# Rows of the earlier expert block fetched during the last block, last block's y added by a gate matrix, in a fused mixer and grouped-MoE layer

## What is computed

```python
    logits = (xt @ w_router).astype(jnp.float32) + router_bias.astype(jnp.float32)
    probs = jax.nn.softmax(logits, axis=-1)
    grp = probs.reshape(-1, N_EXPERT_GROUPS, EXPERTS_PER_GROUP)
    grp_score = lax.top_k(grp, TOP_K)[0].sum(-1)
    g_idx = lax.top_k(grp_score, 1)[1][:, 0]
    ...
    top_w, top_i = lax.top_k(jnp.where(emask, probs, -1.0), TOP_K)
    top_w = top_w / jnp.sum(top_w, axis=-1, keepdims=True)
    ...
    for e in range(N_EXPERTS):
        h = jax.nn.silu(xt @ w_gate[e]) * (xt @ w_up[e])
        y = y + gates[:, e:e + 1] * (h @ w_down[e])
```

## Time and profile before

| what | us |
|---|---|
| median of 3 runs (691.17 to 695.81) | 694.7 |
| the profiled execution | 699.86 |
| its span | 698.0 |
| TensorE busy | 665.8 |
| VectorE busy | 506.0 |
| ScalarE busy | 345.7 |
| GpSimd busy | 133.6 |

### The profile page before, as it was taken

One profiled execution on the slowest core, in us unless ns is written; L12 is line 12 of the kernel. 1 busy time (PEld: TensorE's weight loads), 2 busy tenths in 40 slices (PEclk: granted clock), 3 DMA queues, 4 the chain that ended last, 5 costly groups with the idle time before them and its releaser, 6 DMA issues. The chain is left out here.

```text
span 698.0 us, 9606 instructions
## 1 busy us (share of the span) xinstructions
PE 665.8 (95%) x3815; PEld 560.5 (80%) x3815; DVE 506.0 (72%) x583; ACT 345.7 (50%) x342; POOL 133.6 (19%) x80
## 2 busy tenths in 40 slices
PE   6999999988999999999969999999999999999796
PEld 5999899988997887577858888888888888888531
DVE  4226446799667384767695999999999999999536
ACT  4538412312227241011506787777787777777202
POOL 0000524332031210400020111111111111100064
PEclk9999999999999999999899999999999999999897
DMA  8951111201612105079247999999999999993173
GB/s 285 382 196 61 61 61 61 89 34 61 183 59 86 53 16 193 0 212 413 106 184 285 371 406 397 416 414 411 409 409 406 407 411 414 413 387 116 62 252 132
DMA packets 48689, 162.56 MB, mean 233 GB/s; under 512 B 4294, under 2 KB 23450, under 8 KB 36364
## 3 DMA queue, kind: packets, MB, share of 16 engines
q1 hardware_dynamic: 41756, 136.62, 51.4%
q0 software_dynamic: 6896, 25.43, 9.4%
HBM read 142.61 MB, written 19.44 MB: 232 GB/s over the span
## 5 line engine op out<-in xcount | busy, mean ns | idle before, releaser
L1338 DVE TENSOR_TENSOR RA<-FA,RA 128x2048 fp32r<-128x2048 f32 x93 | 212.9, 2290 | 27.9 <-ACT RA L870 27.2
L870 ACT ACTIVATE RA<-FA 128x2048 fp32r<-128x2048 f32 x93 | 178.9, 1924 | 44.9 <-PE bank L1804 28.8
L1804 PE MATMUL bank<-RA 128*128 128x512 f32 x768 | 185.8, 398 | 2.1 <-DVE RA L1343 2.1
L1804 PEld LDWEIGHTS bank<-RA 128*128 128x128 f32 x768 | 142.3, 190 | 33.4 <-DVE RA L1343 2.4
L1529 PE MATMUL bank<-RA 128*128 128x272 f32 x432 | 111.2, 294 | 0.0
L1530 PE MATMUL bank<-RA 128*128 128x272 f32 x432 | 110.4, 291 | 0.0
L1816 PE MATMUL bank<-RA 128*128 128x512 f32 x384 | 91.6, 395 | 1.4 <-DVE RA L1348 1.4
L1816 PEld LDWEIGHTS bank<-RA 128*128 128x128 f32 x384 | 73.1, 191 | 17.1 <-DVE RA L1348 1.8
L1529 PEld LDWEIGHTS bank<-RA 128*128 128x128 f32 x432 | 83.2, 193 | 0.0
L1530 PEld LDWEIGHTS bank<-RA 128*128 128x128 f32 x432 | 83.1, 192 | 0.0
L994 DVE TENSOR_TENSOR RA<-FA,RA 128x2048 fp32r<-128x2048 f32 (+1 forms) x18 | 48.6, 2700 | 28.1 <-ACT RA L719 27.8
(11 more groups left out here) (246 smaller groups left out, 795.9 us busy)
## 6 DMA issues: line engine op xcount, KB each, us to landing
FA<-w_up SPq DMA_DIRECT2D x32, 1024.0 KB, 7.4
FA<-w_gate SPq DMA_DIRECT2D x32, 1024.0 KB, 6.8
FA<-w_down SPq DMA_DIRECT2D x32, 1024.0 KB, 7.5
FA<-w_in SPq DMA_DIRECT2D x13, 1024.0 KB, 5.0
y_by_slot<-FA POOLq DMA_DIRECT2D x16, 512.0 KB, 7.3
y_by_slot<-FA POOLq DMA_DIRECT2D x1, 4096.0 KB, 17.4
FA<-w_out SPq DMA_DIRECT2D x4, 1024.0 KB, 4.9
FA<-x_prompt SPq DMA_DIRECT2D x8, 256.0 KB, 5.5
```

The costliest lines, as they stand in the source:

```text
L870: nc.scalar.activation(split[split_slot(bi, j)][0], raw[place], ACT.Copy).then_inc(m_hi, 1)
L1338: tt_(sl[1], raw[place], f(sl[0]), ALU.subtract).then_inc(m_lo, 1)
L1804: last = mm(out[:, :], xgT[par][x_][:, kt, :], w[w_][:, t, :], start=(kt == 0 and i == 0), stop=(kt == KT - 1 and i == 2))
```

## The change

It has four parts.

1. Blocks take the experts by their place in the group: block s holds expert 4 * (s % 4) + s // 4 (`expert_at`), so the first four blocks hold place 0 of the four groups, the last four place 3. A token's two rows then lie in two different quarters of the blocks. VectorE sorts each token's two choices by block (`order_slots`: slots, gates `gs_lo`, `gs_hi`, both gates divided by ALPHA), at the start of the experts, behind `overflow_table`, and `x_lo(0, 0)` now comes ahead of both. Two constants for slot counting follow the new order.
2. The lower row (in blocks 0 to 11) is gathered by GpSimd as soon as blocks up to 13 are stored and the last block's raw slots are free, tile 3, 4, 0, 1, 2. Block 14 is stored by SyncE, behind a wait for these five gathers, and the higher row is gathered behind that store. Block 15 is not stored in DRAM at all: its slots in the table are filled with zeros at the start (10 blocks instead of 8).
3. The diagonals and the products with them go. Instead, y_a becomes gate * y_a + x: tiles 0 to 2 on VectorE in one instruction, tiles 3 and 4 scaled by ScalarE (ahead of its copy of h of block 15) and added by GpSimd. y_b becomes gate * y_b + y_a: tiles 0 and 1 on VectorE, tiles 2 to 4 scaled by ScalarE and added by GpSimd. The sum is x + y / ALPHA, and the norm's epsilon is divided by ALPHA squared (`eps_out`).
4. Block 15's y goes to the tokens by a product: VectorE writes, for every token, a row with its gate at its slot of block 15 (`g_tok`), TensorE turns the five tiles into `g_last` (slots by tokens) after blocks 0 and 1 (`turn_gates`), ScalarE copies them. At the end TensorE makes, per tile, g_last times `ysb[1]` and the identity times `y_of(tt, 1)`. ScalarE copies both halves of that y.

The diff, cut to its core (overflow branches left out):

```diff
-SM_E16, SM_G4, SM_VAL, SM_SEQ, SM_TOK, SM_BLK = 0, 16, 20, 25, 33, 38
+SM_E16, SM_G4, SM_VAL, SM_SEQ, SM_TOK, SM_BLK, SM_POS, SM_LEFT = 0, 16, 20, 25, 33, 38, 64, 80
+def expert_at(s, i=0):
+    return 4 * (s % 4) + s // 4 + i
...
-                    load(count_of(s, j) - 1, source(j, bi, bi - 1))
+                    load(count_of(s, j) - 1, source(j, expert_at(s, i), expert_at(s - 1, i)))
...
             moe_loads(E, E, (2, 3))
+            for tt in range(NTT):
+                sp.wait_ge(s_ga[tt][0], 16)
+            sp.wait_ge(m_ya, E - 1)
+            sp.wait_ge(m_yd, E - 1)
+            sp.dma_start(yg_dram.rearrange("(b p) n -> b p n", p=P)[E - 2], ysb[0]).then_inc(s_st14, 16)
...
-            pool.dma_start(yg_dram[E * P:NBLK * P, :].rearrange("(b p) n -> p b n", p=P), fill_src).then_inc(s_fill, 16)
+            pool.dma_start(yg_dram[(E - 2) * P:NBLK * P, :].rearrange("(b p) n -> p b n", p=P), fill_src).then_inc(s_fill, 16)
...
-            store(E - 2, 0)
-            store(E - 1, 1)
-            for par in range(2):
-                pool.wait_ge(m_st[par], 16 * (E // 2))
+            pool.wait_ge(s_sort, 1)
+            pool.wait_ge(m_st[0], 16 * (E // 2 - 1))
+            pool.wait_ge(m_st[1], 16 * (E // 2 - 1))
+            for tt in (3, 4, 0, 1, 2):
+                pool.wait_ge(m_lo, 6 * E - NRAW + 1 + tt // 2)
+                gather_rows(tt, 0)
+            for tt in range(3, NTT):
+                pool.wait_ge(s_scaled, tt - 2)
+                add_scaled(tt, 0, xr[0:rows_of(tt), tt, :])
+            pool.wait_ge(s_st14, 16)
+            pool.wait_ge(m_lo, 6 * E - NRAW + 5)
+            for tt in range(NTT):
+                gather_rows(tt, 1)
...
+            pool.wait_ge(s_xbp, 2)
+            for tt in range(2, NTT):
+                pool.wait_ge(s_scaled, tt + 1)
+                pool.wait_ge(s_xa, 3)
+                add_scaled(tt, 1, y_of(tt, 0))
...
             x_hi(0, 0)
             step(0, 0)
+            act.wait_ge(s_gtt, 1)
+            nc.scalar.activation(g_last[:, 0:SEQ], bank[7][:, :], ACT.Copy).then_inc(s_gc, 1)
             step(1, 1)
+            act.wait_ge(s_gtt, 2)
+            nc.scalar.activation(g_last[:, SEQ:T], bank[7][:, 0:NS], ACT.Copy).then_inc(s_gc, 1)
...
+            def scale_rows(tt, n, gates):
+                act.wait_ge(s_ga[tt][n], 16)
+                nc.scalar.activation(y_of(tt, n), y_of(tt, n), ACT.Copy, scale=gates[0:rows_of(tt), tt:tt + 1]).then_inc(s_scaled, 1)
             mhi(E, 3)
+            scale_rows(3, 0, gs_lo)
+            scale_rows(4, 0, gs_lo)
             h_hi(E - 1)
+            nc.scalar.activation(shift[:, 0:1], eps_ln, ACT.Sqrt)
             y_half(E - 1, 1)
+            nc.scalar.activation(ysb[1][:, 512:D], bank[6][:, :], ACT.Copy).then_inc(m_yd, 1)
...
-            nc.scalar.activation(shift[:, 0:1], eps_ln, ACT.Sqrt)
+            for tt in range(2, NTT):
+                scale_rows(tt, 1, gs_hi)
...
+            x_lo(0, 0)
             overflow_table()
-            x_lo(0, 0)
+            order_slots()
             step(0, 0)
...
-            y_half(E - 1, 1)
+            def add_first(tt, count):
+                dve.wait_ge(s_ga[tt][0], count)
+                stt(y_of(tt, 0), y_of(tt, 0), gs_lo[0:rows_of(tt), tt:tt + 1], xr[0:rows_of(tt), tt, :], ALU.mult,
+                    ALU.add).then_inc(s_xa, 1)
+            for tt in range(3):
+                add_first(tt, 16)
...
-            ts_(diag[:, 0, :], ident, ALPHA, None, ALU.mult).then_inc(s_diag, 1)
-            for tt in range(NTT):
-                rows = P if tt < 4 else NS
-                for n in range(2):
-                    ts_(diag[0:rows, 1 + 2 * tt + n, 0:rows], ident[0:rows, 0:rows],
-                        gw[0:rows, n * NTT + tt:n * NTT + tt + 1], None, ALU.mult).then_inc(s_diag, 1)
+            for tt in range(2):
+                dve.wait_ge(s_ga[tt][1], 16)
+                dve.wait_ge(s_xa, tt + 1)
+                stt(y_of(tt, 1), y_of(tt, 1), gs_hi[:, tt:tt + 1], y_of(tt, 0), ALU.mult, ALU.add).then_inc(s_xbd, 1)
...
             step(0, 0)
+            pe.wait_ge(s_sort, 2)
+            turn_gates(range(4))
             step(1, 1)
+            pe.wait_ge(s_gc, 1)
+            turn_gates((4,))
...
+            pe.wait_ge(s_gc, 2)
             for tt in range(NTT):
...
+                for g, i in enumerate(sum_banks(tt)):
+                    pe.wait_ge((m_ya, m_yd)[g], E)
+                    mm(bank[i][0:rows, :], g_last[:, tok(tt)], ysb[1][:, 512 * g:512 * g + 512], start=True, stop=False)
+                if tt < 2:
+                    pe.wait_ge(s_xbd, tt + 1)
+                else:
+                    pe.wait_ge(s_xbp, tt + 1)
+                for g, i in enumerate(sum_banks(tt)):
+                    last = mm(bank[i][0:rows, :], ident[0:rows, 0:rows], y_of(tt, 1)[:, 512 * g:512 * g + 512],
+                              start=False, stop=True)
                 last.then_inc(s_sum, 1)
```

More of the change, by code:

```diff
@@ L101, in constants @@
     s[:, SM_BLK:SM_BLK + NBLK + 1] = P * np.arange(NBLK + 1)
+    for pos in range(E):
+        s[:, SM_POS + expert_at(pos)] = P * pos
+        s[:, SM_LEFT + expert_at(pos)] = E - pos
     s[:, SM_TOK:SM_TOK + NTT] = np.arange(NTT)[None, :] * P + p[:, None]
@@ L658, in step, with gather_rows, add_scaled @@
                 store(bi - 2, par)
+            def gather_rows(tt, n):
+                pool.indirect_dma_start(
+                    out=y_of(tt, n), out_offset=None, in_=yg_dram,
+                    in_offset=bass.IndirectOffsetOnAxis(ap=slot_i[0:rows_of(tt), 5 * n + tt:5 * n + tt + 1].bitcast(U32), axis=0)).then_inc(s_ga[tt][n], 16)
+            def add_scaled(tt, n, more_):
+                nc.gpsimd.tensor_tensor(y_of(tt, n), y_of(tt, n), more_, ALU.add).then_inc(s_xbp, 1)
             for bi in range(2, E):
                 step(bi, bi % 2)
-            store(E - 2, 0)
-            store(E - 1, 1)
-            for par in range(2):
-                pool.wait_ge(m_st[par], 16 * (E // 2))
+            pool.wait_ge(s_sort, 1)
[9 more added lines that the diff above has]
+            pool.wait_ge(m_lo, 6 * E - NRAW + 5)
+            for tt in range(NTT):
+                gather_rows(tt, 1)
             pool.wait_ge(s_slot, 3)
@@ L1851, in step, with turn_gates @@
                 gate_up(bank[3], par, split_slot(bi, 5), 1, count_of(bi, 5))
+            def turn_gates(tiles):
+                for tt in tiles:
+                    rows, c0 = P if tt < 4 else NS, (tt % 4) * P
+                    last = tr(bank[7][:, c0:c0 + rows], g_tok[0:rows, tt, :], ident[0:rows, 0:rows])
+                last.then_inc(s_gtt, 1)
             keep_clock(28)
```

129 lines of the change are left out of this document (79 added, 50 removed).

## The result

The changed kernel took 684.78 us (median of 4 runs, 683.21 to 689.39) against 694.38 us for the kernel before (4 runs): ratio 0.985, 95% interval 0.980 to 0.989. A later set of 6 runs of it gave 686.22 us and 0.986 (0.983 to 0.989) against 17 runs of before. The forecast was 683.4 us in 678.5 to 690. The profiled execution took 685.86 us, its span 684.0: 14.0 us less than before.

The account below looks back on a forecast made before the run. Bound: weight stream at TensorE's pace until about 633 us, then a serial end. Span 686.1 + 0.6 = 686.7 against 698.0, -11.3; from the 694.7 median, 683.4 us, range 680.5 to 686 (with rivals 678.5 to 690).

Parts of the forecast that it names:

- The stream: Weight loads, splits and products of the expert blocks: kept as they are, new order changes addresses only, cost 0.
- Start of the experts: VectorE's slot sorting and TensorE's gate turns around the first blocks: -0.2 + 0.8 = +0.6 us, between 0 and +2.
- rival B: Row fetches at 3.1 us make GpSimd the bound: 692.8 us, half 688.7; adds may delay TensorE about 1; 0.20 with E.
- One lower fetch per split: During the last block, each lower-row fetch takes one VectorE split of 2.3 us; the five end between 637.3 and 648.4.
- Block 14: Stored at 652 after the lower fetches, landed 654.7; GpSimd adds until 655.3, higher fetches end 656.7 to 661.7.
- TensorE's sum: Gate-matrix and identity products after the last block: start 659.7, 17.2 us plus 0.8 of waiting, end 677.7.
- ScalarE's table between last scaling and first square root: At the end, a 1.28 us load puts the square root at 669.2; VectorE finishes 1.5 us behind TensorE.
- The last 6.9 us: From the last tile's statistics to the end of the span: 6.9 us, ending at 686.1.
- Rival A: At the end, TensorE alone sets the time as fetches land earlier: span 684.1, -13.9, 680.8 us; chance 0.14.
- Rival C: TensorE's clock drops to 1.2 GHz inside the final sum: 1.7 us, nearly all hidden, +0.2, within the forecast.
- D: Weight loads 8 MB apart slow the stream: 2.55 us per cent, gain gone from 4.4%, 703.8 us at 8%; chance 0.03.
- E: Block 13's store lands late, so lower fetches miss the last block: at most rival B minus forecast; 0.20 with B.

Follow-up runs that it names:

- adds behind the fetches: Changed kernel with GpSimd's two adds of x (tiles 3 and 4) moved behind its five higher-row fetches; 689.67 us (a single execution).
- The experiment with one load: Changed kernel with the unused square root that calls ScalarE's table moved behind the overflow branch; 684.67 us, ratio to before 0.987.
- the order of experts alone: Kernel before with only the new order of experts (`expert_at` in loads and counting constants); 694.54 us, ratio 0.999.
- the version with block 14's store free: Changed kernel with all first terms on VectorE, one table load, and block 14 stored without waiting for the lower fetches; 682.68 us, ratio to before 0.983.
- the last version: On top of the version with block 14's store free, tile 4's last operation reads its centred result from PSUM; 684.89 us, ratio 0.985.

## Why the prediction was right

Point by point, with its own terms; times on before's time where they are compared with it.

- **The stream, 0; the fill, 0.** Right: blocks 295.45 and 295.47 with the old and new order, and no row waits for the fill.
- **Start of the experts, +0.6.** Blocks grew by 0.54 us, near the forecast by luck: the sum hides two errors that cancel. The kernel before spent 7.36 us on its last 24 records and a kernel of this change without the collision (adds behind the fetches) 5.74, so before had lost 1.6 us there to the clock; the changed kernel lost about as much (295.99 - 294.41) to a collision of VectorE and GpSimd that the sum had at nothing (rival B below). Free of both, the blocks of before would be 293.8, and the changed ones 294.4: +0.6 is right for the start alone. The gates' turns took 0.60 and 0.24 us where 0.65 and 0.15 were foreseen; the low half of x ended only 0.1 us earlier, not 0.2.
- **One lower fetch per split.** Right to 0.1 us: the last ended at 646.05, 648.3 on before's time, foreseen 648.4. (The first met no split and took 0.98.) All four that stood beside splits behaved like the single row of 2.80. By the rule of the Trainium skill that I weighed there (SBUF — State Buffer, Who interferes with whom) they would have been done by 642; the measurement decided rightly.
- **Block 14.** Store foreseen at 652 and landed at 654.7; it was 651.7, and the first higher fetch started at 655.0. GpSimd's adds were foreseen until 655.3, slowed by the split; they ended at 653.7, and it was the split that was slowed. Higher fetches ended between 656.7 and 661.9, foreseen 656.7 to 661.7. That they go one to a term of VectorE is only half shown: the middle ones took 0.94 + 0.30 us, so near to a term's 1.28 that a held fetch and a free one look alike.
- **TensorE's sum.** Began at 659.7 as foreseen; ended at 677.3 (673.17 + 1.90 + 2.26), foreseen 677.7. It took the 17.2 us plus 0.4; no wait for VectorE's second term is left to see, so the 0.8 us was too much.
- **ScalarE's table between last scaling and first square root.** There, 1.28 us, the square root at 669.1, foreseen 669.2. The order of instructions showed it and the diff did not. VectorE then needed 3.15 us a tile for the 3.28 taken from rows 6, and its last tile started at 678.9 (foreseen 679.2), 1.6 us behind TensorE. The drain of 1.38 us that the Trainium skill (ScalarE: Activation LUTs, What ACT_TABLE_LOAD costs) adds to a switch is not there: the scaling ahead of the load ended at 665.51, the load began at 665.53 and its square root at 666.82. The experiment with one load gave back less than the load itself, not more.
- **The last 6.9 us** were 7.3 (684.0 - 676.67): 0.3 of it is the last operation, 1.54 us for 1.27, with GpSimd's last bias add beside it.
- **Rival A** (TensorE alone sets the end) did not come: VectorE was the 1.6 us later one. **Rival B** did not hold as the bound of GpSimd, but its second half, the order of locks, did: GpSimd's adds started at 646.75, VectorE's last split at 649.13, and the split took 4.46 us; TensorE waited 1.36 us between its two chunks (about 1 was the price given). The rows of before had only GpSimd as the loser; the Trainium skill (SBUF — State Buffer, Who interferes with whom), by which whoever issues first keeps the port, was the better guide, and this trace agrees with it. I should have put it in the sum. **Rival C** (the clock) occurred in before and not in the changed kernel's last block and sum, which hid that price of 1.36 us. **Rivals D and E** are refuted by the order of experts alone and by the first lower fetch at 634.43.
- **The chances** do not add up as written: forecast, A and a third of B make 0.81, not 0.85, and 0.15 is left for a change within 1%. The low end would be 680.8 - 3.5 = 677.3 and not 678.5. Neither bears on the outcome.
- What was not foreseen at all: that ahead of the first turn a kernel varies by over 3 us with the same code. The forecast took a difference read from a single trace off the median, and that the difference of the two stretches is within 0.1 us of it is in part luck; the median came out 1.4 us above the forecast.

## What to carry to other kernels

A serial tail of store, landing, fetch and use is shortened by two things together: fetch what is old while the last block still computes, and let the last block's result reach its users on chip, by a product with a small matrix; here either alone, with the rest of the change in place, brought two fifths of the gain of both at most. When work is moved beside a busy engine, ask who holds the port and who waits behind it, and read the instruction order for table loads that a branch puts in. Where the time ahead of a change varies by a good part of what the change gives, compare the traces between two fixed points of the program and leave the medians for the verdict.

## What the runs showed of the hardware

- VectorE and GpSimd took turns whole, in the order in which they began, where both read two SBUF tensors. The last split took 4.46 to 4.49 us behind GpSimd's adds (four profiles) and 2.28 without them. An operation with one operand in PSUM kept its 1.40 beside the same adds, where that with both in SBUF took 1.92 (2.52 in the version with the adds behind the fetches).
- A row fetch that met a split of VectorE ended 0.8 us behind it, whatever its start. The same holds for one that met a scalar_tensor_tensor of two SBUF tensors. In the version with block 14's store free the first higher fetch ended at 652.60 (650.86 + 1.74), 0.8 us behind the first of these four (650.51 + 1.28 = 651.79):

```profile
650.51 4.90 DVE L1501 SCALAR_TENSOR_TENSOR FA<-FA 128x1024 f32<-128x1024 f32 x4
```

- The clock: with the same two waits in front (0.78 and 1.41 us), 24 records took 7.36, 7.21 and 7.11 us in three profiles and 5.71 to 5.74 in four. By microseconds, the kernel before had from 652 to 655, and the last version from 649 to 652:

```profile
652.00:655.00 3.00, 3.00 (x8) 0.50 0.00 0
```

```profile
649.00:652.00 3.00, 2.53 (x6) 0.50 0.59 239
```

  That is 1.2 GHz instead of 2.4. What decides it stays open: DMA was idle in the one and busy in the other, and the version with block 14's store free had the same waits at full clock.
- A store of 512 KB by SyncE, block 14's, landed in 2.6 to 3.6 us on empty queues (six profiles; 3.1 in the changed kernel) and in 5.5 and 5.4 us with row fetches in flight (two profiles).
